# A depthwise convolution on GpSimd: each tap's product and sum in two halves of the row, in turn

## The chip, the cores and the metric

The kernel runs on one core of a Trainium2 chip. The metric is the device time of one execution in microseconds (us). A core has five engines that run their own instruction queues in order and meet only through semaphores: TensorE (PE), VectorE (DVE), ScalarE (ACT), GpSimd (POOL) and SyncE (SP), which here only issues transfers. Lower is better.

## The reference

One decoder layer over 1024 tokens of width 1024. An input projection feeds three mixers side by side: sparse attention (an indexer picks 256 keys for each query, then softmax attention), multi-scale pooling, and a convolution module. Their outputs are concatenated, projected, normalised, and go through a mixture of experts (top 2 of 16) with a second norm. The part that matters here is the convolution module on 256 channels, 31 taps wide:

```python
def conformer_conv(u, conv_w, conv_b, ln_g, ln_b):
    a, gate = jnp.split(u, 2, axis=-1)
    h = a * jax.nn.sigmoid(gate)
    h = lax.conv_general_dilated(h, conv_w, window_strides=(1,), padding=[(CONV_WIDTH - 1, 0)], ...
                                 feature_group_count=D_C) + conv_b
    h = layer_norm(h, ln_g, ln_b)
    return jax.nn.silu(h)
```

Each channel is filtered on its own: output(t) is the bias plus the sum over w of weight(w) times h(t + w - 30). Everything is float32.

## The kernel before, in words

Channels lie on partitions, tokens along the free dimension, so a tap w is a shifted read of a padded row: hpad[:, g, w:w + 1024] times one weight per partition. There are two groups g of 128 channels. Their inputs hpad are set by VectorE at the end of the input projection (L1393), and the result is conv[:, g, :], 1024 elements a partition.

Group 0: TensorE does taps 0 to 23 as matmuls with diagonal matrices (L740), ScalarE brings the result with the bias to conv[:, 0, :] (L1148, semaphore conv0), and GpSimd adds taps 24 to 30 (L1910 a product into the buffer tapped, L1911 a sum into conv; semaphore conv0_rest counts the sums).

Group 1: GpSimd does all 31 taps in the helper tap(w). Tap 0 is one instruction with product and bias (L1875). Taps 1 to 30 are a product into tapped (L1878) and a sum into conv (L1879), whose semaphore is conv1. The helper link() lets the engine wait for the instruction just issued. The product of tap w waits for the sum of tap w - 1, since it overwrites tapped, and the sum waits for its product.

GpSimd's queue in order: causal masks (L1859), taps 0 to 7 of group 1, the pooling mixer (L1885 to L1903), taps 8 to 30 of group 1, taps 24 to 30 of group 0, small tables for the router (L1916 to L1926), and much later the gathers and scatters of the experts and the additions of the last norm (L1986).

Beside the taps three things run. First the end of the projection with VectorE's split L1350 and 25 rounds of a search for the top-k threshold (L1444). Then, from about 250 us, the attention proper, whose order of steps is written out by attention_steps(): "qk" scores (TensorE L786), VectorE's bias and row maximum (L1532), ScalarE's exponential (L1155), transposes (TensorE L806, copies by ScalarE L1163 or VectorE L1541), and the product with the values (TensorE L819, ScalarE L1167). Between them VectorE fits seven "choose" instructions for each block of queries (L1476 to L1488) that turn the scores into a mask; several have two inputs in SBUF.

Who waits for the taps: near the end of the attention steps stand "split 0" and "cm". In "split 0" ScalarE waits for conv0_rest and conv1 (L1142, L1143) before it casts a first piece of mix (L1119). In "cm" TensorE waits for both (L838, L839) and sums conv over the channels for its norm (L841). VectorE then subtracts the mean (L1556). The steps behind them in each queue (the scores and products of the last pairs, and then the output projection) wait in order.

Of the kernel before, what the change touches and what calls it, by code (L numbers as in the profile page):

```python
# [17 lines left out]
S, D = 1024, 1024  # L18
# [4 lines left out]
TAPS = 31  # L23
# [47 lines left out]
TAPS_PE = 24  # L71
# [140 lines left out]
def program(nc, a):  # L212
    ctx = ExitStack()
    with ctx:
# [5 lines left out]
        def sem(name):  # L220
            return ctx.enter_context(nc.semaphore(name))
# [178 lines left out]
        def probs_at(u):  # L400
# [21 lines left out]
            sem(n) for n in ("diag_set", "conv0_mm", "conv0", "conv1", "pooled", "pool_chain"))  # L422
        conv0_rest, both_in, both_mm = sem("conv0_rest"), sem("both_in"), sem("both_mm")

# [219 lines left out]
        def _(pe):  # L644
# [116 lines left out]
            for step in STEPS:  # L761
# [46 lines left out]
                elif kind == "pv":  # L808
                    _, b, j, n = step
# [26 lines left out]
                elif kind == "cm":  # L836
                    _, c, r = step
                    pe.wait_ge(conv0_rest, TAPS - TAPS_PE)  # L838
                    pe.wait_ge(conv1, TAPS)  # L839
                    for i in range(2):  # L840
# [174 lines left out]
        def _(act):  # L1015
# [109 lines left out]
            for step in STEPS:  # L1125
# [14 lines left out]
                elif kind == "split":  # L1140
                    if step[1] == 0:
                        act.wait_ge(conv0_rest, TAPS - TAPS_PE)  # L1142
                        act.wait_ge(conv1, TAPS)  # L1143
                        act.wait_ge(ring_act, seen(RING_ACT, RING_OF["pw", 1, 1]))
# [698 lines left out]
        def _(pool):  # L1843
# [23 lines left out]
            def link(ins):  # L1867
                own[0] += 1
                ins.then_inc(pool_chain, 1)
                pool.wait_ge(pool_chain, own[0])  # L1870

            def tap(w):
                src, by = hpad[:, 1, w:w + S], convw[:, TAPS + w:TAPS + w + 1]
                if w == 0:
                    pool.tensor_scalar(conv[:, 1, :], src, by, convb[:, 1:2], ALU.mult, ALU.add).then_inc(conv1, 1)  # L1875
                else:
                    pool.wait_ge(conv1, w)
                    link(pool.tensor_scalar(tapped[:], src, by, None, ALU.mult))  # L1878
                    pool.tensor_tensor(conv[:, 1, :], conv[:, 1, :], tapped[:], ALU.add).then_inc(conv1, 1)  # L1879

# [26 lines left out]
            pool.wait_ge(conv0, 1)  # L1907
            pool.wait_ge(conv1, TAPS)
            for n, w in enumerate(range(TAPS_PE, TAPS)):
                link(pool.tensor_scalar(tapped[:], hpad[:, 0, w:w + S], convw[:, w:w + 1], None, ALU.mult))  # L1910
                pool.tensor_tensor(conv[:, 0, :], conv[:, 0, :], tapped[:], ALU.add).then_inc(conv0_rest, 1)  # L1911
                pool.wait_ge(conv0_rest, n + 1)

# [133 lines left out]
```

## Time and profile before

| | us |
|---|---|
| median of 3 runs (lowest to highest) | 1001.8 (1001.33 to 1005.58) |
| the profiled execution, whole | 1005.54 |
| its span, first to last instruction | 1003.6 |
| TensorE busy in the span | 912.2 (91%) |
| VectorE busy | 695.6 (69%) |
| ScalarE busy | 560.6 (56%) |
| GpSimd busy | 370.0 (37%) |
| GpSimd, products of taps L1878 and L1910 | 92.0 + 22.6 |
| GpSimd, sums of taps L1879 and L1911 | 74.4 + 17.8 |

The page's strip cuts the span into 40 slices of 25 us; a digit is the busy share in tenths:

```profile
PE   6999999999798789999936999999999999999980
DVE  5339888798899956636677767798888854334276
POOL 0000079999999992000001112122232221111136
PEclk9999999999899999999978999999999999999995
```

TensorE is nearly full all along; the stretch of GpSimd's taps is slices 6 to 16, about 130 to 381 us. An average over the span says little about a change of GpSimd's work; what counts is the stretch in which it runs and who waits for its end.

### The profile page before, as it was taken

Reading aid. Unit: us, or ns where it says so; the run is one execution under the profiler, and the core shown is the slowest. Engines: PE = TensorE matmul, PEld = TensorE weight load, DVE = VectorE, ACT = ScalarE, POOL = GpSimd, SP = SyncE. Lnnn points to the kernel's source line nnn. Section 1 sums busy time; section 2 is a strip of 40 time slices with the busy share of each in tenths; the row PEclk is TensorE's granted clock in tenths of the full one; section 3 lists DMA queues with packets and bytes.
Section 4 is the critical chain, followed back from the end, with each engine's and each line's share of the span. In section 5 each row is a group of like instructions: output and inputs, shape, how many; then the busy total and the mean of one; then the engine's idle time right before and its main releaser. Section 6 shows DMA issues by size and latency. Waiting matters only on the chain.

```text
span 1003.6 us, 15909 instructions
## 1 busy us (share of the span) xinstructions
PE 912.2 (91%) x4804; PEld 715.4 (71%) x4805; DVE 695.6 (69%) x1028; ACT 560.6 (56%) x805; POOL 370.0 (37%) x243
## 2 busy tenths in 40 slices
PE   6999999999798789999936999999999999999980
PEld 5877888744366567888825888888878888888760
DVE  5339888798899956636677767798888854334276
ACT  4256667686687566611141656778777744234342
POOL 0000079999999992000001112122232221111136
PEclk9999999999899999999978999999999999999995
DMA  8550111000000100242685679999999987652375
GB/s 234 135 141 22 42 43 64 1 0 2 1 1 1 44 1 22 93 151 69 256 335 210 214 221 330 383 400 403 384 403 396 391 293 248 199 146 43 107 243 206
DMA packets 63486, 172.54 MB, mean 172 GB/s; under 512 B 19297, under 2 KB 33633, under 8 KB 51120
## 3 DMA queue, kind: packets, MB, share of 16 engines
q1 hardware_dynamic: 55664, 143.85, 38.8%
q0 software_dynamic: 7488, 27.07, 10.9%
q10 hardware_dynamic: 288, 1.05, 0.3%
q8 instruction: 24, 0.39, 0.2%
q14 instruction: 22, 0.18, 0.1%
HBM read 142.79 MB, written 26.74 MB: 169 GB/s over the span
## 4 chain that ended last, share of the span: by engine, by line
PE 51%; DMA 4%; DVE 3%; issue 2%; ACT 2%; POOL 1%; DVEq 0%; POOLq 0%; ACTq 0%; SPq 0%
PE ps L467 14%; PE ps L469 14%; PE ps L468 14%; DMA raw<-in_w_gate 3%; PE ps L946 2%; PE ps L819 1%; PE ps L786 1%; POOL xb L1986 1%; PE ps L982 1%; PE ps L870 1%; DMA acc_d<-ysb,idx_add 1%; PE ps L806 1%; DVE xgT_lo L1761 0%; DVE wlo L1751 0%; DMA xg<-x_d,slot_token 0%
## 5 line engine op out<-in xcount | busy, mean ns | idle before, releaser
L1751 DVE TENSOR_TENSOR wlo<-raw,whi 128x2048 fp32r<-128x2048 f32 x96 | 216.2, 2288 | 52.1 <-ACT whi L1245 52.1
L1245 ACT CAST whi<-raw 128x2048 fp32r<-128x2048 f32 x96 | 180.2, 1911 | 48.2 <-PE ps L469 18.5
L467 PE MATMUL ps<-whi,xgT_hi 128*128 128x512 f32 x384 | 152.5, 397 | 6.2 <-DVE xgT_lo L1761 6.2
L469 PE MATMUL ps<-whi,xgT_lo 128*128 128x512 f32 x384 | 150.6, 392 | 0.0
L468 PE MATMUL ps<-wlo,xgT_hi 128*128 128x512 f32 x384 | 150.2, 391 | 0.0
L1878 POOL TENSOR_SCALAR tapped<-hpad,par 128x1024 f32<-128x1024 f32 x30 | 92.0, 3067 | 2.9
L467 PE MATMUL ps<-xT_hi,w_hi 128*128 128x512 f32 (+1 forms) x224 | 88.0, 393 | 1.9 <-DVE xT_lo L1357 1.9
L1954 POOL COPY idx_now<-slot_token 128x1 int32 (+1 forms) x24 | 8.1, 336 | 219.9 <-PE ps L946 219.9
L467 PEld LDWEIGHTS ps<-whi,xgT_hi 128*128 128x128 f32 x384 | 72.7, 189 | 22.4 <-issue 6.4
L468 PE MATMUL ps<-xT_lo,w_hi 128*128 128x512 f32 (+1 forms) x224 | 86.7, 387 | 0.0
L469 PE MATMUL ps<-xT_hi,w_lo 128*128 128x512 f32 (+1 forms) x224 | 86.6, 387 | 0.0
L469 PEld LDWEIGHTS ps<-whi,xgT_lo 128*128 128x128 f32 x384 | 72.5, 189 | 15.4
L468 PEld LDWEIGHTS ps<-wlo,xgT_hi 128*128 128x128 f32 x384 | 72.5, 189 | 14.5
L467 PE MATMUL ps<-whi,hT_hi 128*128 128x512 f32 x192 | 76.9, 401 | 0.5 <-issue 0.5
L1444 DVE TENSOR_SCALAR_CACHE_REDUCE junk_dve<-bias,sm 128x1024 bf16<-128x1024 f32 (+2 forms) x75 | 75.7, 1010 | 1.8
L1879 POOL TENSOR_TENSOR conv<-conv,tapped 128x1024 f32<-128x1024 f32 x30 | 74.4, 2480 | 2.5
L469 PE MATMUL ps<-whi,hT_lo 128*128 128x512 f32 x192 | 75.1, 391 | 0.0
L468 PE MATMUL ps<-wlo,hT_hi 128*128 128x512 f32 x192 | 74.9, 390 | 0.0
L1969 POOL DMA_INDIRECT acc_d<-ysb,idx_add x23 | 40.3, 1751 | 93.2 <-ACT ysb L1272 92.4
L1095 ACT ACTIVATE junk_act<-bias,sm 128x768 bf16<-128x768 f32 (+2 forms) x75 | 62.2, 829 | 14.7 <-DVE sm L1462 10.6
L1532 DVE CUSTOM_DVE_ANT_0 probs<-ps,bias 128x128 f32<-128x128 f32 (+7 forms) x64 | 45.9, 754 | 20.2 <-PE ps L786 17.5
L1155 ACT ACTIVATE probs<-probs,sm 128x128 f32<-128x128 f32 (+7 forms) x64 | 50.0, 781 | 14.0 <-DVE sm L1532 14.0
(328 smaller groups left out, 1818.4 us busy)
## 6 DMA issues: line engine op xcount, KB each, us to landing
raw<-in_w_gate SPq DMA_DIRECT2D x32, 1024.0 KB, 10.4
raw<-in_w_up SPq DMA_DIRECT2D x32, 1024.0 KB, 11.7
raw<-in_w_down SPq DMA_DIRECT2D x32, 1024.0 KB, 9.4
w_raw<-in_w_in SPq DMA_DIRECT2D x14, 512.0 KB, 3.9
x_tok<-in_x SPq DMA_DIRECT2D x8, 512.0 KB, 7.7
wo_raw<-in_w_o SPq DMA_DIRECT2D x16, 256.0 KB, 2.8
x_res<-in_x SPq DMA_DIRECT2D x16, 256.0 KB, 3.4
x_d<-xa SPq DMA_DIRECT2D x4, 512.0 KB, 6.1
```

Of the source, the lines that this page charges most:

```text
L467: pe.matmul(out, l_hi, r_hi, start=start, stop=False)
L468: pe.matmul(out, l_hi, r_lo, start=False, stop=False)
L469: return pe.matmul(out, l_lo, r_hi, start=False, stop=stop)
L1095: act.activation(junk_act[:, 0:WIDTH[b]], bias[:, AT[b]:AT[b] + WIDTH[b]], ACT.Sign, bias=cands[r % 2][:, c:c + 1], scale=-1.0, accum_out= ...
L1155: act.activation(row, row, ACT.Exp, bias=negmax[:, c:c + 1], scale=-1.0, accum_out=rowsum[:, c:c + 1]).then_inc(exped, 1)
L1245: act.copy(whi[:, n, :], raw[:, n, :]).then_inc(gu_hi if n < 4 else dn_hi, 1)
L1444: dve.tensor_scalar(junk_dve[:, 0:WIDTH[b]], bias[:, AT[b]:AT[b] + WIDTH[b]], now[:, c:c + 1], 0.0, ALU.is_lt, ALU.add, accum_out=res[:, c ...
L1532: dve.tensor_tensor_reduce(out=probs_at(u)[:, 0:WIDTH[b]], in0=scores_at(u, WIDTH[b]), in1=bias[:, AT[b]:AT[b] + WIDTH[b]], scale=-1.0, sc ...
L1751: dve.tensor_tensor(wlo[:, n, :], raw[:, n, :], f32(whi[:, n, :]), ALU.subtract).then_inc(gu_lo if n < 4 else dn_lo, 1)
L1878: link(pool.tensor_scalar(tapped[:], src, by, None, ALU.mult))
L1879: pool.tensor_tensor(conv[:, 1, :], conv[:, 1, :], tapped[:], ALU.add).then_inc(conv1, 1)
L1969: pool.indirect_dma_start(acc_d, bass.IndirectOffsetOnAxis(ap=idx_add[:], axis=0), ysb[:], None, compute_op=ALU.add).then_inc(y_out, 16)
```

## The change

Each tap but the 0th is done in two halves of 512 elements. Where there was one product and one sum, there are now product of half 0, product of half 1, sum of half 0, sum of half 1. A product of half c waits for the sum of half c of the tap before; a sum of half c waits for its own product. All of them count on two semaphores: tap_mul for products, conv1 for sums (tap 0 adds 2 to it, both groups count on it). The semaphore conv0_rest is gone, and the consumers wait for conv1 at its final value.

```diff
@@ TensorE, step "cm" @@
-                    pe.wait_ge(conv0_rest, TAPS - TAPS_PE)
-                    pe.wait_ge(conv1, TAPS)
+                    pe.wait_ge(conv1, 2 * (2 * TAPS - TAPS_PE))
@@ ScalarE, step "split" 0 @@
-                        act.wait_ge(conv0_rest, TAPS - TAPS_PE)
-                        act.wait_ge(conv1, TAPS)
+                        act.wait_ge(conv1, 2 * (2 * TAPS - TAPS_PE))
@@ GpSimd, tap(w) @@
                 if w == 0:
-                    pool.tensor_scalar(conv[:, 1, :], src, by, convb[:, 1:2], ALU.mult, ALU.add).then_inc(conv1, 1)
+                    pool.tensor_scalar(conv[:, 1, :], src, by, convb[:, 1:2], ALU.mult, ALU.add).then_inc(conv1, 2)
                 else:
-                    pool.wait_ge(conv1, w)
-                    link(pool.tensor_scalar(tapped[:], src, by, None, ALU.mult))
-                    pool.tensor_tensor(conv[:, 1, :], conv[:, 1, :], tapped[:], ALU.add).then_inc(conv1, 1)
+                    for c in range(2):
+                        half = slice(c * 512, (c + 1) * 512)
+                        pool.wait_ge(conv1, 2 * w - 1 + c)
+                        pool.tensor_scalar(tapped[:, half], src[:, half], by, None, ALU.mult).then_inc(tap_mul, 1)
+                    for c in range(2):
+                        half = slice(c * 512, (c + 1) * 512)
+                        pool.wait_ge(tap_mul, 2 * w - 1 + c)
+                        pool.tensor_tensor(conv[:, 1, half], conv[:, 1, half], tapped[:, half], ALU.add).then_inc(conv1, 1)
@@ GpSimd, taps 24 to 30 of group 0 @@
-            pool.wait_ge(conv1, TAPS)
+            pool.wait_ge(conv1, 2 * TAPS)
             for n, w in enumerate(range(TAPS_PE, TAPS)):
-                link(pool.tensor_scalar(tapped[:], hpad[:, 0, w:w + S], convw[:, w:w + 1], None, ALU.mult))
-                pool.tensor_tensor(conv[:, 0, :], conv[:, 0, :], tapped[:], ALU.add).then_inc(conv0_rest, 1)
-                pool.wait_ge(conv0_rest, n + 1)
+                for c in range(2):
+                    half = slice(c * 512, (c + 1) * 512)
+                    pool.wait_ge(conv1, 2 * (TAPS + n) - 1 + c)
+                    pool.tensor_scalar(tapped[:, half], hpad[:, 0, w + c * 512:w + (c + 1) * 512], convw[:, w:w + 1],
+                                       None, ALU.mult).then_inc(tap_mul, 1)
+                for c in range(2):
+                    half = slice(c * 512, (c + 1) * 512)
+                    pool.wait_ge(tap_mul, 2 * (TAPS + n) - 1 + c)
+                    pool.tensor_tensor(conv[:, 0, half], conv[:, 0, half], tapped[:, half], ALU.add).then_inc(conv1, 1)
```

## Rows read from the trace of the kernel before

**Rows 1.** Busy time by engine in one stretch (start:end, length, then each engine):

```profile
255.00:357.00 102.00, 84.51 (x720) 55.46 (x718) 96.73 (x160) 69.94 (x188) 98.83 (x35) 0.95 0.04 12
```

The engines are PE, PEld, DVE, ACT and POOL, each with its number of instructions; then PEclk, the DMA share and GB/s.

**Rows 2.** Timeline of GpSimd: start, duration (us), line, operation, out<-in.

```profile
130.63 1.19 POOL L1875 TENSOR_SCALAR conv<-hpad,par 128x1024 f32<-128x1024 f32 x1 [0.28 <-DVE hpad L1393]
...
213.58 2.84 POOL L1878 TENSOR_SCALAR tapped<-hpad,par 128x1024 f32<-128x1024 f32 x1
216.50 2.36 POOL L1879 TENSOR_TENSOR conv<-conv,tapped 128x1024 f32<-128x1024 f32 x1
218.96 2.84 POOL L1878 TENSOR_SCALAR tapped<-hpad,par 128x1024 f32<-128x1024 f32 x1
...
378.48 2.38 POOL L1911 TENSOR_TENSOR conv<-conv,tapped 128x1024 f32<-128x1024 f32 x1
380.94 0.22 POOL L1916 TENSOR_TENSOR fold<-ident 128x16 f32<-128x16 f32 x1
381.10 0.31 POOL L1917 MEMSET rw_wide<- 128x256 f32 x1
```

**Rows 3.** Timelines of TensorE and ScalarE where the taps' end is needed.

```profile
382.52 3.60 PE L841 MATMUL ps<-conv,ones_conv 128*128 128x512 f32 x8
...
383.00 1.04 ACT L1119 CAST mix_hi<-mix 128x1024 fp32r<-128x1024 f32 x1
```

**Rows 4.** GpSimd's groups by line: count | busy us, mean ns | idle before.

```profile
L1878 POOL TENSOR_SCALAR tapped<-hpad,par 128x1024 f32<-128x1024 f32 x30 | 92.0, 3067 | 2.9
L1879 POOL TENSOR_TENSOR conv<-conv,tapped 128x1024 f32<-128x1024 f32 x30 | 74.4, 2480 | 2.5
...
L1910 POOL TENSOR_SCALAR tapped<-hpad,par 128x1024 f32<-128x1024 f32 x7 | 22.6, 3231 | 0.8 <-POOL conv L1879 0.2
L1911 POOL TENSOR_TENSOR conv<-conv,tapped 128x1024 f32<-128x1024 f32 x7 | 17.8, 2538 | 0.6
...
L1899 POOL TENSOR_TENSOR doubled<-doubled,par 64x16 f32<-64x16 f32 x4 | 0.9, 216 | 0.3
...
L1925 POOL TENSOR_TENSOR rw_gain<-sm 128x128 f32<-128x128 f32 x1 | 0.4, 400 | 0.1
```

**Rows 5.** Timeline of GpSimd near the end: sums that don't wait for each other.

```profile
983.34 9.28 POOL L1986 TENSOR_TENSOR xb<-xb,ln_b 128x1024 f32<-128x1024 f32 x4
992.59 2.34 POOL L1986 TENSOR_TENSOR xg<-xg,ln_b 128x1024 f32<-128x1024 f32 x1
```

**Rows 6.** Timelines of VectorE and GpSimd over the same microseconds, in two places.

```profile
285.12 1.54 DVE L1480 SCALAR_TENSOR_TENSOR tied<-bias,sm,above 128x640 f32<-128x640 f32 x1
...
342.78 4.33 DVE L1482 TENSOR_TENSOR_SCAN tie_no<-tied 128x1024 f32<-128x1024 f32 x1
...
349.29 1.24 DVE L1484 SCALAR_TENSOR_TENSOR tied<-tie_no,sm,tied 128x1024 f32<-128x1024 f32 x1
350.56 3.26 DVE L1486 SCALAR_TENSOR_TENSOR tied<-tied,above 128x1024 f32<-128x1024 f32 x1
...
284.87 2.85 POOL L1878 TENSOR_SCALAR tapped<-hpad,par 128x1024 f32<-128x1024 f32 x1
...
345.06 4.70 POOL L1910 TENSOR_SCALAR tapped<-hpad,par 128x1024 f32<-128x1024 f32 x1
349.84 2.90 POOL L1911 TENSOR_TENSOR conv<-conv,tapped 128x1024 f32<-128x1024 f32 x1
```

**Rows 7.** VectorE's groups by line from 250 to 358 us.

```profile
L1486 DVE SCALAR_TENSOR_TENSOR tied<-tied,above 128x512 f32<-128x512 f32 (+5 forms) x6 | 11.6, 1928 | 0.1
L1480 DVE SCALAR_TENSOR_TENSOR tied<-bias,sm,above 128x512 f32<-128x512 f32 (+5 forms) x6 | 10.4, 1738 | 0.0
...
L1484 DVE SCALAR_TENSOR_TENSOR tied<-tie_no,sm,tied 128x512 f32<-128x512 f32 (+5 forms) x6 | 9.4, 1564 | 0.0
```

**Rows 8.** TensorE busy and its granted clock (PEclk, third number) in two windows.

```profile
328.00:332.00 4.00, 1.05 (x6) 0.92 0.00 0
332.00:336.00 4.00, 4.00 (x32) 0.65 0.01 4
```

More of the change, by code:

```diff
@@ L422, in program @@
             sem(n) for n in ("diag_set", "conv0_mm", "conv0", "conv1", "pooled", "pool_chain"))
-        conv0_rest, both_in, both_mm = sem("conv0_rest"), sem("both_in"), sem("both_mm")
+        tap_mul, both_in, both_mm = sem("tap_mul"), sem("both_in"), sem("both_mm")
         ring_mm, ring_act, ring_dve = sem("ring_mm"), sem("ring_act"), sem("ring_dve")
```

## The prediction

> **What bounds the kernel now.** I read the page's slices first and then one stretch, that of GpSimd's taps. GpSimd's strip is full from about 130 to 381 us and nearly empty elsewhere, so the change can act there alone. In the window over the attention part [rows 1] the reader is to see that from 255 to 357 us GpSimd is busy 98.8 of 102 us and VectorE 96.7, while TensorE has 84.5 and ScalarE 69.9: in this stretch VectorE (its scores, maxima and top-k choices) holds the pace and TensorE idles some 17 us. Behind that, on the page's chain of work, TensorE's matmuls follow each other with hardly a piece of another engine.
>
> The timeline of GpSimd [rows 2] shows the taps as one unbroken chain: a first tap at 130.63 us, then product and sum in strict turn, each waiting for the one before, until the last sum ends at 378.48 + 2.38 = 380.86 us. Who needs that end is in the code: TensorE's "cm" step (L838 to L841, sums over the convolved channels) and ScalarE's first "split" wait for all 37 products and sums, and each stands in order in its queue. The timeline of both [rows 3] shows TensorE's first L841 matmul at 382.52 us and ScalarE's cast at 383.00, neither behind a wait. The slack of the taps is thus 382.52 - 380.86 = 1.66 us: anything that lengthens GpSimd's chain by more is paid one for one by TensorE, and shortening it gives nothing beyond what TensorE itself can use. From 382 us on the chain that ended last is TensorE's nearly everywhere, and the transfers of the experts' weights are issued on events behind this point, so I let a shift at 382 us go through to the end undiminished.
>
> **The change, part by part.** It removes 37 products and 37 sums of 1024 elements a partition (30 taps on the second channel group, 7 on the first) and adds 74 of each at 512. A half's product now waits for the same half's sum of the tap before, and a sum for its own half's product, so that the instruction just ahead is never the one waited for. The 0th tap, the pooling between taps and the bytes moved stay.
>
> Step 1, a tap today. Undisturbed, 213.58 to 218.96 us is 5.38 us [rows 2]: product 2.84, gap 0.08, sum 2.36, gap 0.10. These are gaps of a dependent pair.
>
> Step 2, half lengths. The sum's fixed part comes from short ones [rows 4]: 16 elements take 216 ns, so 2360 ns at 1024 is 2.13 ns an element and 182 ns fixed; from the 128-element row (400 ns) the fixed part is 120 ns. Half a sum is 1.24 to 1.27 us. The single-operation product has no short row. I give it the sum's fixed 0.18 us, so half is 1.42 + 0.09 = 1.51 us; the bounds are none at all and nearly two thirds of it, see the third rival. Four instructions: 3.02 + 2.54 = 5.56 us.
>
> Step 3, the gaps. Where GpSimd's instructions don't wait for each other, the next starts before the last ends: the four sums of the last norm and the fifth start over 992.59 - 983.34 = 9.25 us, 2.31 each, with a duration of 2.34 [rows 5], an overlap of 0.03; the short pair at 380.94 and 381.10 overlaps by 0.06 [rows 2]. Four boundaries save 0.13 to 0.24 us beside the 5.56. A tap is then 5.32 to 5.43 us, 5.26 with the smaller fixed part: -0.12 to +0.05 us against today. I take the middle, -0.02, because the short and the long pair bound it evenly: 37 x -0.02 = -0.7 us, ends -4.4 and +1.9 us (no overlap at all would be +6.7). So the removed wait is worth about what the added starts cost.
>
> Step 4, the meeting with VectorE. The rows [rows 6] show the two engines in each other's way: VectorE's L1486 over 1024 elements took 3.26 us from 350.56, while the same kind of instruction, L1484, took 1.24 at 349.29. Its own 1.24 us can have begun only at 350.56 + 3.26 - 1.24 = 352.58, and the GpSimd sum it had met ran from 349.84 to 352.74. In turn GpSimd's product at 345.06 took 4.70 in place of 2.84, since the scan at 342.78 (4.33 us, itself held up by a sum) ran until 347.11. L1484 at 349.29 ran free beside the late part of that product (to 349.76), while L1480 at 285.12, over 640 elements, took 1.54 us where 0.78 would do: it got through at 285.88, 1.0 us after the start of the product at 284.87. So a sum blocks VectorE's two-input instructions for nearly all its time, a product only in its early part. The Trainium skill says the same more strictly (SBUF — State Buffer, Who interferes with whom): the loser waits for the whole instruction of the other. The trace agrees for sums and not for products.
> What this costs GpSimd today: the mean durations [rows 4] less the undisturbed 2.84 and 2.36 give 30 x (0.223 + 0.120) + 7 x (0.387 + 0.178) = 14.2 us. What it costs VectorE: the three three-operand groups [rows 7] are busy 31.4 us; 18 instructions over 3 x 4224 elements at 1.24 us per 1024 would be 15.3, so 16 us of waiting on these alone, more with the scans.
> With halves a VectorE instruction that meets a sum waits for half a sum, so its waits should fall to about half, 8 us or more off a stretch in which it sets the pace. GpSimd loses: today a VectorE instruction of about 1 us often fits into the 1.9 us in which a product leaves the way free; with two free pieces of about 0.95 us each it overruns into the next read. Over a tap's cycle I get 0.35 us of delay for each such instruction today and 0.54 after. With some 35 instructions that is +6.6 us; the even arrival it assumes is not what the rows show (VectorE's instructions queue up behind GpSimd's), so I take +5, bounds 0 and +8.
>
> Step 5, the sum. GpSimd's end moves by -0.7 + 5 = +4.3 us. Less 1.66 of slack, TensorE's cm step is 2.6 us late against today. VectorE's gain does not help: it brings TensorE to that step perhaps 8 us early, where it waits in order, with qk and pv of the next pair queued behind, and ScalarE behind its own wait. That idle time has a price: behind an idle piece (1.05 busy of 4 us) the granted clock was 0.92 and then 0.65 over 4 us in which TensorE was full [rows 8], 1.7 us lost in all. The cm matmuls would meet the same, +1.7 us, bounds 0 and their own 3.6 us [rows 3]. Together 2.6 + 1.7 = +4.3 us.
>
> The profiled execution took 1005.54 us, span 1003.6; changed it would be 1009.8. The runs have their median at 1001.8, 3.7 us below it; I carry the difference over unchanged: 1001.8 + 4.3 = 1006.1 us. The same difference says that the slack of 1.66 us may be smaller in other runs, if they are quicker ahead of 382 us.
>
> **The rivals.**
> First, the taps end earlier. If starts overlap by more than 0.06 us at half length and VectorE delays GpSimd no more than today, the tap is up to 0.2 us shorter and the end 0 to 7 us earlier. The slack (-1.66) and the clock's price (+1.7) cancel, so the kernel gains what GpSimd's end gains: VectorE's freed time has TensorE there early enough to use it. For it: VectorE is the pace setter and loses over 16 us to whole sums. Against it: step 3's overlaps are small. Time 995 to 1001.8 us; it decides from the point where the shorter tap outweighs the added delay by VectorE, 0.14 us a tap for +5.
> Second, on the slow side: VectorE finds no opening. Today every GpSimd instruction is followed by a gap in which a blocked VectorE instruction gets in. If back-to-back halves leave none, it waits through Sa, Sb and a product's read instead of one sum, its waits double (+16 us and more on the groups of [rows 7]), and TensorE reaches cm late. Place: L1480 to L1488 between 255 and 357 us; it decides once the extra waits pass TensorE's 17 us of idleness there, or GpSimd's end. Time 1011 to 1026 us. No row shows back-to-back GpSimd reads beside such VectorE instructions.
> Third, the product's cost isn't in its length. The 0th tap, a product with an added bias over the same 1024 elements, took 1.19 us [rows 2], the plain product 2.84. If the plain one also moves its data in 1.0 us, some 1.8 are fixed, a half takes 2.3 us, a tap is 1.7 us longer and 37 of them are +63 us: about 1065 us. Against it: L1480 found the way shut for the product's first 1.0 us [rows 6], so the reading stands at its start, which a fixed part ahead of the data would not give; a fixed part behind it isn't excluded. The Trainium skill (GPSIMD Engine Reference, Engine selection) calls one-input operations roughly line-rate, which speaks for this rival; the row of 2.84 us disagrees.
> Fourth, the change doesn't do what it says: the halves follow each other with today's dependent gaps of 0.09 us. A tap is 5.56 + 0.36 = 5.92, 37 x 0.54 = +20 us: about 1022 us.
>
> **How the numbers follow.** Forecast 57%: GpSimd ends 0 to 9 us later, 1001.8 to 1011; of that 20 points lie over +5 us. First rival 24%, of which 13 points are faster by over 5 us. Second 8%, third 6%, fourth 5%. A change under 0.5% (5 us) can hardly be told from none here, since three runs spread over 4 us. Faster 0.13, same 0.37 + 0.11 = 0.48, slower 0.20 + 0.19 = 0.39. The range goes from 996.0, which leaves out 9 of the first rival's points, to 1021, which leaves out the third rival and 5 points of the second and fourth: 20 in all.
>
> **What would show it.** GpSimd's lines: 74 products near 1.51 us and 74 sums near 1.27 undisturbed, four starts in 5.3 to 5.4 us; a product near 2.3 is the third rival, gaps of 0.09 the fourth. GpSimd's last half sum near 385 us, TensorE's L841 starting within 0.2 us of it behind a wait on it, of some 10 us, at a granted clock below 1. L1480 to L1488 busy 8 us less or more confirms step 4, more busy than today is the second rival. The forecast is wrong if L841 isn't behind the taps, or if the part behind 390 us doesn't take its time of today.

## The result, and the profile after

| | before | after |
|---|---|---|
| median, us | 1002.6 (4 runs, 1001.33 to 1005.58) | 1014.2 (4 runs, 1013.87 to 1015.66) |
| ratio, 95% interval | | 1.0109 [1.0085, 1.0133] |
| profiled execution, its span | 1005.54, 1003.6 | 1013.87, 1011.5 |
| first tap starts | 130.63 | 127.63 |
| last sum of the taps ends | 380.86 | 388.21 |
| first cm matmul starts | 382.52, behind no wait | 388.35, behind a wait of 17.97 |

The changed kernel is slower by 1.1%. One execution of those that follow, of whole rows with the product ahead, ran with TensorE's granted clock at 0.555 throughout and took 1559.42 us; it is left out of the ratios. In the changed kernel the lines have moved by a few: products are L1878 and L1916, sums L1882 and L1921, the cm matmuls L840, ScalarE's first cast L1118, VectorE's choose instructions L1474 to L1486.

The slices of the page after, to be held against the four rows of before: GpSimd's strip is full from slice 6 to 15 and has a 4 in slice 16 where it had a 2, and TensorE's has a 5 and a 6 in slices 15 and 16 (about 354 to 405 us) where it had an 8 and a 9.

```profile
PE   6999999999899856999955999999999999999990
DVE  5249888898899633637678766698988854334276
POOL 0000099999999994000001112123133221111237
PEclk9999999999999987899976999999999999999995
```

The timeline of GpSimd after (start, duration, line, operation; x2 is two instructions printed as one row, an undisturbed tap being two such rows, and the last rows are the end of the taps) answers to [rows 2]:

```profile
127.63 1.20 POOL L1873 TENSOR_SCALAR conv<-hpad,par 128x1024 f32<-128x1024 f32 x1 [0.35 <-DVE hpad L1391]
...
207.46 3.11 POOL L1878 TENSOR_SCALAR tapped<-hpad,par 128x512 f32<-128x512 f32 x2
210.53 2.51 POOL L1882 TENSOR_TENSOR conv<-conv,tapped 128x512 f32<-128x512 f32 x2
213.00 3.11 POOL L1878 TENSOR_SCALAR tapped<-hpad,par 128x512 f32<-128x512 f32 x2
216.08 2.51 POOL L1882 TENSOR_TENSOR conv<-conv,tapped 128x512 f32<-128x512 f32 x2
218.56 1.57 POOL L1878 TENSOR_SCALAR tapped<-hpad,par 128x512 f32<-128x512 f32 x1
...
349.36 3.11 POOL L1916 TENSOR_SCALAR tapped<-hpad,par 128x512 f32<-128x512 f32 x2 [0.16 <-POOL conv L1882]
...
385.71 2.50 POOL L1921 TENSOR_TENSOR conv<-conv,tapped 128x512 f32<-128x512 f32 x2
```

The two taps from 207.46 to 218.56 us take 5.55 us each, where one took 5.38 [rows 2]. That is the first thing to see: the tap is longer even where nothing disturbs it. The second is the start of both chains: the profiled execution of before had its first tap 3.0 us later than the one of after. So the end of the taps moved by 388.21 - 380.86 = 7.35 us on the page, but the chain itself grew from 380.86 - 130.63 = 250.23 to 388.21 - 127.63 = 260.58 us, by 10.35.

GpSimd's groups after, from 120 to 400 us (count | busy us, mean ns of one | idle before), answer to [rows 4]:

```profile
L1878 POOL TENSOR_SCALAR tapped<-hpad,par 128x512 f32<-128x512 f32 x60 | 101.6, 1705 | 0.2
L1882 POOL TENSOR_TENSOR conv<-conv,tapped 128x512 f32<-128x512 f32 x60 | 83.8, 1418 | 0.0
L1916 POOL TENSOR_SCALAR tapped<-hpad,par 128x512 f32<-128x512 f32 x14 | 21.9, 1582 | 0.2 <-POOL conv L1882 0.2
L1921 POOL TENSOR_TENSOR conv<-conv,tapped 128x512 f32<-128x512 f32 x14 | 17.6, 1285 | 0.0
```

The timelines of TensorE and of ScalarE after, where they need the taps, answer to [rows 3]:

```profile
369.72 0.66 PE L827 MATMUL ps<-ident,rlrep 128*128 128x128 f32 x4
388.35 6.05 PE L840 MATMUL ps<-conv,ones_conv 128*128 128x512 f32 x8 [17.97 <-POOL conv L1921]
394.33 1.99 PE L786 MATMUL ps<-keyT,qT 64*128 64x512 f32 x8
...
388.24 1.04 ACT L1118 CAST mix_hi<-mix 128x1024 fp32r<-128x1024 f32 x1 [17.44 <-POOL conv L1921]
```

TensorE stood at cm from 370.38 us, 12.1 us earlier than in [rows 3], and waited 17.97 us. Its eight matmuls then took 6.05 us in place of 3.60. The windows over this place (start:end, length, then PE, PEld, DVE, ACT and POOL with their counts, PEclk, DMA share, GB/s; the first window is that of [rows 1]):

```profile
255.00:357.00 102.00, 92.27 (x812) 62.70 (x812) 84.14 (x159) 76.09 (x199) 101.84 (x65) 0.97 0.04 12
...
370.00:388.00 18.00, 0.38 (x4) 0.14 (x2) 1.21 (x2) 0.81 (x2) 18.00 (x14) 0.57 0.00 0
388.00:392.00 4.00, 3.65 (x5) 1.61 (x6) 2.16 (x2) 1.56 (x2) 3.35 (x9) 0.50 0.02 4
392.00:396.00 4.00, 4.00 (x13) 1.46 (x11) 2.57 (x4) 0.00 (x0) 0.00 (x0) 0.86 0.21 66
396.00:400.00 4.00, 3.68 (x46) 3.02 (x44) 2.66 (x5) 1.73 (x4) 0.00 (x0) 1.00 0.00 0
```

Two things stand in them. In the first window VectorE is busy 84.1 us where it was 96.7, and TensorE 92.3 where it was 84.5 [rows 1]: that part of the kernel did get quicker. And the clock is at 0.50, the lower of TensorE's two levels (1.2 GHz), while the engine is full from 388 us, and back at 1.00 from 396.

VectorE's groups after, from 250 to 358 us, answer to [rows 7]:

```profile
L1480 DVE TENSOR_TENSOR_SCAN tie_no<-tied 128x512 f32<-128x512 f32 (+5 forms) x6 | 11.9, 1984 | 0.1
L1484 DVE SCALAR_TENSOR_TENSOR tied<-tied,above 128x512 f32<-128x512 f32 (+5 forms) x6 | 8.7, 1454 | 0.1
L1482 DVE SCALAR_TENSOR_TENSOR tied<-tie_no,sm,tied 128x512 f32<-128x512 f32 (+5 forms) x6 | 7.6, 1273 | 0.0
L1478 DVE SCALAR_TENSOR_TENSOR tied<-bias,sm,above 128x512 f32<-128x512 f32 (+5 forms) x6 | 7.0, 1161 | 0.0
```

The three three-operand groups are busy 8.7 + 7.6 + 7.0 = 23.3 us, where they were 31.4.

### The profile page after: what moved, and what is told of

The parts are those of the page before. It is cut to its first block, busy times and chain, and to the rows that moved or that the text cites. A ratio compares the mean times of both kernels' runs of the same rounds, so it can differ in the third digit from the quotient of the medians.

```text
span 1011.5 us, 15981 instructions
## 1 busy us (share of the span) xinstructions
PE 911.8 (90%) x4804; PEld 716.1 (71%) x4805; DVE 684.6 (68%) x1028; ACT 560.6 (55%) x805; POOL 387.4 (38%) x317
## 3 DMA queue, kind: packets, MB, share of 16 engines
q0 software_dynamic: 7488, 27.07, 10.9%
q10 hardware_dynamic: 288, 1.05, 0.3%
## 4 chain that ended last, share of the span: by engine, by line
PE 50%; POOL 26%; DMA 11%; DVE 7%; issue 3%; ACT 2%; DVEq 0%; ACTq 0%; POOLq 0%; SPq 0%
PE ps L467 14%; PE ps L469 14%; PE ps L468 14%; POOL tapped L1878 10%; DMA raw<-in_w_gate 10%; POOL conv L1882 8%; POOL tapped L1916 2%; DVE wlo L1749 2%; POOL conv L1921 2%; PE ps L945 1%; POOL doubled L1896 1%; DVE bias L1403 1%; POOL doubled L1903 1%; PE ps L711 1%; DVE sm L1595 1%
## 5 line engine op out<-in xcount | busy, mean ns | idle before, releaser
L1878 POOL TENSOR_SCALAR tapped<-hpad,par 128x512 f32<-128x512 f32 x60 | 101.6, 1705 | 0.2
L1882 POOL TENSOR_TENSOR conv<-conv,tapped 128x512 f32<-128x512 f32 x60 | 83.8, 1418 | 0.0
L468 PEld LDWEIGHTS ps<-wlo,xgT_hi 128*128 128x128 f32 x384 | 72.2, 188 | 14.2
L1094 ACT ACTIVATE junk_act<-bias,sm 128x768 bf16<-128x768 f32 (+2 forms) x75 | 62.2, 829 | 15.1 <-DVE sm L1460 11.1
L1260 ACT ACTIVATE silu<-ps 128x512 f32<-128x512 f32 x24 | 14.3, 595 | 76.6 <-PE ps L469 76.6
```

The lines of the kernel that those rows point to most:

```text
L468: pe.matmul(out, l_hi, r_lo, start=False, stop=False)
L1094: act.activation(junk_act[:, 0:WIDTH[b]], bias[:, AT[b]:AT[b] + WIDTH[b]], ACT.Sign, bias=cands[r % 2][:, c:c + 1], scale=-1.0, accum_out= ...
L1878: pool.tensor_scalar(tapped[:, half], src[:, half], by, None, ALU.mult).then_inc(tap_mul, 1)
L1882: pool.tensor_tensor(conv[:, 1, half], conv[:, 1, half], tapped[:, half], ALU.add).then_inc(conv1, 1)
```

## The experiments

The first theory, from these rows: the length of GpSimd's chain sets the end, since it is 10 us longer while TensorE comes 9 us earlier (12.1 less the 3.0 us of the earlier start); what VectorE wins from the halves is real, but is spent waiting at cm. Its rival: the slower time comes from elsewhere (more instructions, the clock, VectorE), and the wait at cm only shows it. A second question is why VectorE wins: because a half is short, or because of the order in which the halves come.

Where a table or a text below says "three groups" it is the busy time of the three groups above from 250 to 358 us, and "cm after the first tap" is the start of the first cm matmul less that of the first tap, which takes the early or late start of an execution out.

**The load on GpSimd and TensorE.** One constant was changed, in the kernel before and in the one after: TensorE does three more taps of group 0 and GpSimd three fewer.

```diff
-TAPS_PE = 24
+TAPS_PE = 27
```

On the changed kernel:

> The changed kernel with 27 in place of 24 taps of group 0 on TensorE, 4 instead of 7 on GpSimd. Theory A (the changed kernel lost because GpSimd's end holds up step cm by 18 us, while VectorE's freed time had TensorE there 9 us early): GpSimd ends 3 x 5.56 = 16.7 us earlier, TensorE has 6 matmuls of 0.45 us more, it waits next to nothing, and the time falls by 16 us to about 998 us, 4 to 6 us below the kernel before. Rival (the halves cost elsewhere too, not only at this wait): the time stays above 1003 us.

On the kernel before:

> Control to the run with 27 taps: the kernel before with the same three taps moved from GpSimd to TensorE. Theory A (TensorE was not waiting for GpSimd, its pace up to 357 us is VectorE's, which whole-length sums hold up): GpSimd ends 16 us earlier without use, TensorE has 2.7 us more matmuls just ahead of the scores, so 1002 to 1005 us, minus at most 3 us by less meeting of GpSimd and VectorE near 355 us. Rival (GpSimd's end held this kernel too): 3 us or more faster than before.

The first took 1000.73 us, ratio to before 0.9974 [0.9952, 0.9996]; the second 1010.99 us, ratio 1.0064 [1.0036, 1.0091]. The timeline of TensorE shows the cm matmuls of the first at 374.85 us, at their undisturbed 3.6 us and without a wait, as GpSimd's last sum had ended at 370.5. So taking away three taps took 13.5 us off the changed kernel: the wait at cm is its price, and the first theory holds. The same edit made the kernel before slower, though GpSimd was done at 359.4 us, 29 us ahead of cm at 388.0: it gained nothing from an earlier end and paid for the taps on TensorE, with VectorE's three groups at 32.5 us. That is a miss upward, as 1002 to 1005 us had been expected: the last tap matmuls ahead of the attention (L740) take 15.73 us for 36 where they took 10.58 for 24, so the three taps cost TensorE 5.2 us there and not 2.7. Cm is 8.2 us later after the first tap than in the kernel before; where the other 3 us went wasn't looked into. Eight of the ten executions took 1010.7 to 1013.1 us and two 1003.3 and 1004.4, and why isn't known. The pair is also the cleanest measure of what the halves give VectorE, since in neither do the taps hold anything up: cm comes 247.2 us after the first tap with halves and 260.1 without, and the kernel is 0.9% faster.

**The order of the halves.** Product, sum, product, sum, each waiting for the one ahead of it, so that only the lengths are those of the change:

```diff
                     for c in range(2):
                         half = slice(c * 512, (c + 1) * 512)
-                        pool.wait_ge(conv1, 2 * w - 1 + c)
+                        pool.wait_ge(conv1, 2 * w + c)
                         pool.tensor_scalar(tapped[:, half], src[:, half], by, None, ALU.mult).then_inc(tap_mul, 1)
-                    for c in range(2):
-                        half = slice(c * 512, (c + 1) * 512)
                         pool.wait_ge(tap_mul, 2 * w - 1 + c)
```

> Halves as in the changed kernel, but in the order product, sum, product, sum, each waiting for the instruction just ahead. It tells what the interleaving is worth apart from the length. Theory A (added starts cost 6.4 us, the interleaving only hides a gap of about 0.12 us at each of 4 boundaries): an undisturbed tap of 5.56 + 4 x 0.12 = 6.0 us, GpSimd's end 37 x 0.48 = 18 us behind that of the changed kernel, time 1014 + 17 = 1031 us. Theory B (the interleaving matters for more, since dependent halves open the way to VectorE between any two): the tap is 6.0 us too, but VectorE's three-operand groups are faster than in the changed kernel by some us more. Rival: the waits cost nothing and the tap stays 5.56 us, time 1014 us.

1029.34 us, ratio 1.0254 [1.0221, 1.0287]. The timeline of GpSimd in this kernel:

```profile
213.71 1.57 POOL L1878 TENSOR_SCALAR tapped<-hpad,par 128x512 f32<-128x512 f32 x1
215.36 1.27 POOL L1880 TENSOR_TENSOR conv<-conv,tapped 128x512 f32<-128x512 f32 x1
216.73 1.56 POOL L1878 TENSOR_SCALAR tapped<-hpad,par 128x512 f32<-128x512 f32 x1
218.38 1.27 POOL L1880 TENSOR_TENSOR conv<-conv,tapped 128x512 f32<-128x512 f32 x1
219.75 1.56 POOL L1878 TENSOR_SCALAR tapped<-hpad,par 128x512 f32<-128x512 f32 x1
```

The same four instructions take 6.04 us instead of 5.55: gaps of 0.08 and 0.10 us stand where the changed kernel overlaps by 0.03. So the interleaving does what it says, 0.49 us a tap. In this order a tap in halves costs 0.66 us more than a whole one (6.04 against 5.38), and the interleaving hides three quarters of it. VectorE's three groups are busy 24.3 us here, nearly the 23.3 of the changed kernel. With these products it is the length of the halves that frees VectorE, not their order.

**The interleaving alone, with whole rows.** Products and sums of 1024 elements, with three buffers for products, so that from tap 8 on a product is issued ahead of the sum it doesn't need. The core of the edit:

```diff
+            def product(n):
+                g, w = todo[n]
+                if n > 2:
+                    pool.wait_ge(conv1, TAPS_FIRST + n - 2)
+                pool.tensor_scalar(ahead[n % 3][:], hpad[:, g, w:w + S], ...
+                                   None, ALU.mult).then_inc(tap_mul, 1)
...
+                pool.tensor_tensor(conv[:, g, :], conv[:, g, :], ahead[n % 3][:], ALU.add).then_inc(conv1, 1)
```

> The kernel before, whole lengths, but from tap 8 on with three product buffers and each product issued one ahead of the sum before it, so that no instruction waits for the one just ahead (30 of 37 taps). It isolates the wait that the change wanted to hide. Theory A (an independent start saves 0.10 to 0.13 us at each of two boundaries): tap 5.38 - 0.24 = 5.14 us undisturbed, GpSimd's end 7 us earlier, near 371 us when it starts at 128, and the time that of before, 1000 to 1004 us, since TensorE didn't wait for it. Rival (without gaps VectorE finds no opening between whole instructions): VectorE's three-operand groups busier than 31 us, TensorE late at step cm, 1006 us or more.

1004.47 us, ratio 1.0002 [0.9967, 1.0036]. The rows are those of another run of the same kernel:

> The kernel with products one ahead once more, for a profile at TensorE's usual clock. Theory A (a removed wait is worth 0.12 us a boundary, and TensorE didn't wait for GpSimd): undisturbed tap 5.14 us, step cm without a wait, some 1003 us. Rival (the gaps were VectorE's openings): three-operand groups of VectorE busier than their 31 us of the kernel before, and step cm later by as much.

One time, 1003.81 us. A tap takes 5.15 us in it (213.20 to 218.35), 0.23 less than before, the last sum ends at 373.6 and the cm matmuls start at 380.8, behind no wait. The gaps are gone and GpSimd is done 7 us ahead of cm, and the kernel isn't faster: VectorE's three groups are busy 32.8 us (31.4 before), and cm comes 253.1 us after the first tap (251.9 before). A shorter chain on GpSimd is worth nothing by itself here.

**The product's cost.** The prediction's third rival turned on tap 0, a product with an addition that took 1.19 us while the plain product took 2.84. Here every product, whole as before, also adds 0.0:

```diff
-                    link(pool.tensor_scalar(tapped[:], src, by, None, ALU.mult))
+                    link(pool.tensor_scalar(tapped[:], src, by, 0.0, ALU.mult, ALU.add))
```

> The kernel before with one edit: each product is multiply, then add 0.0, in place of multiply alone; whole length. Tap 0, which multiplies and adds, took 1.19 us for the 1024 elements for which the plain product takes 2.84. Theory A (the two-operation form has a quicker path): product 1.2 us, a tap of 3.7, GpSimd's end 37 x 1.65 = 61 us earlier, near 320 us. TensorE's step cm is then nowhere near waiting, and the kernel gains only what VectorE gets back in its stretch, up to the 17 us of TensorE's idle time there: 990 to 1000 us. Rival (tap 0 is quick because both of its scalars come from memory, or because its source is aligned): product 2.84 us as before, time 1002 us.

998.22 us, ratio 0.9952 [0.9928, 0.9975]. GpSimd's timeline in this kernel:

```profile
210.14 2.36 POOL L1879 TENSOR_TENSOR conv<-conv,tapped 128x1024 f32<-128x1024 f32 x1
212.60 1.12 POOL L1878 TENSOR_SCALAR tapped<-hpad,par 128x1024 f32<-128x1024 f32 x1
213.80 2.35 POOL L1879 TENSOR_TENSOR conv<-conv,tapped 128x1024 f32<-128x1024 f32 x1
```

The product takes 1.12 us. The taps end at 312.7 us, 68 us sooner than before, and the kernel gains 5. VectorE's three groups are at 26.4 us: it meets none of GpSimd's instructions after 313. Up to there its waits are no shorter than before: what the 18 instructions of the three groups took over their undisturbed lengths is an estimated 11 us, all of it ahead of 313, where the kernel before has 10 us ahead of 313 and 6 behind.

**Both together.** The changed kernel with the quick products:

```diff
-                        pool.tensor_scalar(tapped[:, half], src[:, half], by, None, ALU.mult).then_inc(tap_mul, 1)
+                        pool.tensor_scalar(tapped[:, half], src[:, half], by, 0.0, ALU.mult, ALU.add).then_inc(tap_mul, 1)
```

> The changed kernel (halves in turn) with each product as multiply, then add 0.0. Theory A (both effects are separate: the quick form takes GpSimd's end out of the way, halves shorten VectorE's waits): half products of 0.65 us, a tap of 3.7 to 3.8 us, GpSimd's end near 330 us, TensorE at step cm near 370 us without a wait as in the changed kernel (370.4), so 9 us under before: about 993 us, and 4 us under whole-length quick products. Rival (VectorE gains nothing further, since quick products leave less of GpSimd's time free between sums): 998 us, that of the whole-length quick products.

1006.02 us, ratio 1.0036 [1.0014, 1.0058]. That is a miss: slower than whole rows with the same products (0.9952), although the taps end at 323.5 us and no one waits for them. VectorE's three groups are busy 30.1 us. A timeline of VectorE and one of GpSimd over the same microseconds in this kernel show one of its long waits:

```profile
282.97 2.81 DVE L1484 SCALAR_TENSOR_TENSOR tied<-tied,above 128x384 f32<-128x384 f32 x1
...
281.06 1.75 POOL L1878 TENSOR_SCALAR tapped<-hpad,par 128x512 f32<-128x512 f32 x2
282.79 2.49 POOL L1882 TENSOR_TENSOR conv<-conv,tapped 128x512 f32<-128x512 f32 x2
285.25 1.75 POOL L1878 TENSOR_SCALAR tapped<-hpad,par 128x512 f32<-128x512 f32 x2
```

L1484 over 384 elements takes 0.51 us undisturbed (L1486 at 275.60 us in the trace of before). Here it took 2.81, so it worked from 285.27 on: it had waited through both half sums, 282.79 to 285.28, and got in only as the products began. Three more of the 18 instructions of the three groups waited 2.2 us or more in this way, at 256.33, 261.26 and 278.19 us. This is the prediction's second rival, VectorE finding no opening between two instructions that follow without a gap. The test for it is to put the gaps back, with the quick products kept: the chained order of the first experiment and the addition of 0.0.

> Halves with quick products (multiply, then add 0.0), in the order product, sum, product, sum, each waiting for the one just ahead. Beside it stand the same halves in turn (1006 us), where VectorE's two-input instructions waited 2.2 to 2.8 us, longer than a half. Theory A (back-to-back halves pass the way on to each other when products are short; a dependent gap opens it to VectorE): no wait of VectorE's much over 1.3 us, its five choose groups 10 us less busy than in that run, GpSimd's end near 340 us and harmless, TensorE at cm near 370 us: 991 to 996 us, the fastest so far. Rival (short products themselves are at fault, since they leave VectorE fewer free stretches): the groups stay as busy, 1002 to 1007 us.

997.28 us, ratio 0.992 [0.989, 0.995]. The three groups fall from 30.1 to 22.6 us, and cm comes 243.9 us after the first tap instead of 253.5, though each tap is longer, 4.29 us against 3.80. That this costs GpSimd half a microsecond a tap doesn't matter, since the taps end at 346.0.

But the edit changes two things at once: it puts a gap behind each half, and it parts the two sums by a product. No run here has the one without the other, so which of them lets VectorE in is not shown. More rows of the kernel without gaps, VectorE and then GpSimd, in two places:

```profile
153.14 7.55 DVE L1348 TENSOR_TENSOR w_lo<-w_raw,w_hi 128x1024 fp32r<-128x1024 f32 x1 [0.61 <-ACT w_hi L1019]
...
153.22 2.55 POOL L1882 TENSOR_TENSOR conv<-conv,tapped 128x512 f32<-128x512 f32 x2
155.74 1.37 POOL L1878 TENSOR_SCALAR tapped<-hpad,par 128x512 f32<-128x512 f32 x2
157.07 2.54 POOL L1882 TENSOR_TENSOR conv<-conv,tapped 128x512 f32<-128x512 f32 x2
...
315.88 1.68 DVE L1482 SCALAR_TENSOR_TENSOR tied<-tie_no,sm,tied 128x768 f32<-128x768 f32 x1
...
315.49 1.26 POOL L1921 TENSOR_TENSOR conv<-conv,tapped 128x512 f32<-128x512 f32 x1
316.71 1.98 POOL L1921 TENSOR_TENSOR conv<-conv,tapped 128x512 f32<-128x512 f32 x1
```

L1348 takes 1.23 us where nothing is in its way. Here it ended at 160.69, so it had waited 6.3 us, past two half sums, two products and two more half sums: the products between the sums did not let it in, which speaks for the gap. Against a rule without exception stands L1482 at 315.88 us. It needs about 0.95 us, so it worked from about 316.6 on, as the first half sum ended, and the second half sum grew from 1.27 to 1.98 us: VectorE got in between two sums that had no gap.

**More taps on GpSimd.** The freed time of GpSimd can take taps from TensorE. With TAPS_PE = 18, on halves in the change's order and on whole rows, both with quick products:

> As the run before it, but with 18 taps of group 0 on TensorE and 13 on GpSimd. Theory A (27 taps on TensorE cost 5 us of its time in front of the attention, and GpSimd now has some 40 us to spare): GpSimd's end 6 x 3.75 = 22 us later, near 353 us, still ahead of cm; TensorE loses 12 matmuls of 0.45 us, 5.4 us, just in front of the scores: about 987 us. Rival (VectorE's search, done near 247 us, sets the start of the attention): within 2 us of the run before it.

> The kernel before, whole lengths, quick products, 18 taps on TensorE. With the run before it, it tells what halves are worth once GpSimd is out of the way. Theory A (halves shorten VectorE's waits): 4 us above the run before it, about 991 us. Rival (halves worth nothing here): the same time as that run.

1007.56 us, ratio 1.0046 [1.0018, 1.0074], and 1002.55 us, ratio 1.0004 [0.9982, 1.0027]: two misses by 20 and 12 us. On whole rows it is slower than with 24 taps (0.9952); on halves the intervals overlap (1.0036 with 24). GpSimd then works longer beside VectorE's choose instructions (three groups 31.4 and 31.5 us), and TensorE stood for 7.7 us in either behind ScalarE's conv0 (L1146 and L1148), which the shorter work of TensorE had it reach early. With TAPS_PE = 22, chained halves and then whole rows:

> The run before it with 22 taps of group 0 on TensorE, 9 on GpSimd. In the run with whole quick products ScalarE waited 2.88 us for TensorE's taps before it could bring the convolution out, while with 18 taps TensorE waited for ScalarE instead. Two taps fewer take 1.8 us off TensorE there: 1 to 2 us under the run before it. Rival: less than 0.5 us, if the search's end sets the start anyway, or 1 to 2 us more, if the 9 us of added GpSimd work meet VectorE's choose instructions.

> Whole rows, products as a multiply and an addition of 0.0, no halves, and TAPS_PE = 22 in place of 24 (two more taps of a channel tile on GpSimd than in the kernel before). Against e10, which has the same products, the same 22 and chained halves, only the length of GpSimd's instructions differs. Tap 3.66 us by e2's trace, against 4.29 in the chained halves: GpSimd has more room here than there. Theory A (short instructions with a gap behind each give VectorE its openings, and that is what e9 had over e2): VectorE's groups of three-operand instructions keep their waits (31 us or more for the three largest after the scan, e10 had 22.8), the search is later, and the time is 2 to 4 us over e10's: 996 to 998. Rival (the halves gained nothing, TensorE's load set e10's time): 992 to 995, GpSimd being done earlier. Decides between them: the ratio against e10's 0.989, and VectorE's groups in the stretch from 250 to 358.

993.44 us, ratio 0.9889 [0.9848, 0.9929], the fastest of all here, and 997.37 us, ratio 0.9937 [0.9918, 0.9957]. VectorE's groups in the chained halves, and then on whole rows, show the difference between them:

```profile
L1484 DVE SCALAR_TENSOR_TENSOR tied<-tied,above 128x512 f32<-128x512 f32 (+5 forms) x6 | 8.2, 1370 | 0.1
L1482 DVE SCALAR_TENSOR_TENSOR tied<-tie_no,sm,tied 128x512 f32<-128x512 f32 (+5 forms) x6 | 8.2, 1362 | 0.0
L1478 DVE SCALAR_TENSOR_TENSOR tied<-bias,sm,above 128x512 f32<-128x512 f32 (+5 forms) x6 | 6.4, 1074 | 0.0
```

```profile
L1486 DVE SCALAR_TENSOR_TENSOR tied<-tied,above 128x512 f32<-128x512 f32 (+5 forms) x6 | 9.9, 1651 | 0.1
L1484 DVE SCALAR_TENSOR_TENSOR tied<-tie_no,sm,tied 128x512 f32<-128x512 f32 (+5 forms) x6 | 9.1, 1516 | 0.0
L1480 DVE SCALAR_TENSOR_TENSOR tied<-bias,sm,above 128x512 f32<-128x512 f32 (+5 forms) x6 | 8.4, 1403 | 0.0
```

22.8 us against 27.4, and cm 239.8 against 248.3 us after the first tap. The 31 us that the theory asked for on whole rows weren't reached, the time of 996 to 998 was. The two intervals overlap a little, so the 4 us between the medians rest on these rows as much as on the times. Whether 22 is better than 24 with chained halves (0.9889 against 0.992) the runs don't tell: the intervals overlap widely.

The profiled executions side by side. P and S are product and sum, "dep" that each instruction waits for the one ahead:

| kernel | tap, us | taps end | three groups | cm after first tap | ratio |
|---|---|---|---|---|---|
| before (whole, dep) | 5.38 | 380.9 | 31.4 | 251.9 | 1 |
| after (halves PPSS) | 5.55 | 388.2 | 23.3 | 260.7, waited 18.0 | 1.0109 |
| after, 27 taps on TensorE | 5.54 | 370.5 | 22.0 | 247.2 | 0.9974 |
| before, 27 | 5.39 | 359.4 | 32.5 | 260.1 | 1.0064 |
| halves PSPS, dep | 6.04 | 408.4 | 24.3 | 277.4, waited 33.0 | 1.0254 |
| whole, product ahead | 5.15 | 373.6 | 32.8 | 253.1 | 1.0002 |
| quick, whole, dep | 3.66 | 312.7 | 26.4 | 246.5 | 0.9952 |
| quick, halves PPSS | 3.80 | 323.5 | 30.1 | 253.5 | 1.0036 |
| quick, halves PSPS, dep | 4.29 | 346.0 | 22.6 | 243.9 | 0.992 |
| the same, 22 taps on TensorE | 4.29 | 357.2 | 22.8 | 239.8 | 0.9889 |
| quick, whole, dep, 22 | 3.66 | 322.8 | 27.4 | 248.3 | 0.9937 |
| quick, halves PPSS, 18 | 3.80 | 351.9 | 31.4 | 255.9 | 1.0046 |
| quick, whole, dep, 18 | 3.66 | 338.9 | 31.5 | 251.8 | 1.0004 |

Only where cm waited do the taps decide. Of the rest, those with 30 us or more in the three groups reach cm 251.8 us or more after the first tap, those with 27.4 or less within 249.

## Why the prediction was right or wrong

The time lies in the range, the sign of the forecast was right, and so was the chain of reasons: the taps' end is what the change lengthens, VectorE's gain brings TensorE to cm early, it waits there, and the clock falls. The size was too small: +4.3 us forecast, +11.6 between the medians (the ratio gives +10.9). That the time lies in the range is in part luck: the forecast's own band was 1001.8 to 1011 us, and 1014.2 lies above it, in the band of the second rival (1011 to 1026), which isn't what made this kernel slower. By its steps:

**Slack at cm.** 1.66 us, used as the forecast said. Chain +10.35, less 1.66, plus 2.45 for the cm matmuls, is +11.1 us. The profiled spans differ by 7.9; with the 3.0 us by which the taps of before began later it is 10.9. So the sum closes, and nothing behind cm gave time back, as had been assumed. What the prediction had taken from this was wrong in one point: it carried the 3.7 us between the profiled execution and the median over to the changed kernel, and feared that the slack might be smaller in quick executions. The profiled execution of before lost 3.0 us ahead of its first tap. That moves the taps' end and TensorE's arrival at cm alike and leaves the slack as it is, and the changed kernel's profiled execution had no such loss (1013.87 us, its median 1014.2).

**Steps 2 and 3, the tap in halves: this is the step that failed.** It said -0.02 us a tap, -0.7 in all, with ends of -4.4 and +1.9 and +6.7 if nothing overlapped. It is +0.17 a tap, 37 x 0.17 = +6.3. Two terms were mis-sized. The product's fixed part was taken from the sum, 0.18 us, for want of a short product; it is 2 x 1.57 - 2.84 = 0.30, which is 0.12 us a tap. And the overlap of neighbours is 0.03 us each (3.11 for two of 1.57), the lower of the two rows it was taken between; the middle of both had been used, 0.07 us a tap too much. (The middle of the prediction's own -0.12 and +0.05 is -0.035 and not -0.02; that is 0.6 us over 37 taps, and to the wrong side.) Together 0.19 x 37 = 7.0 us, nearly the whole miss. The half sum, 1.27 us, was right.

**Step 4, the meeting with VectorE.** For VectorE: 8 us or more off the three groups was forecast, 8.1 came. For GpSimd: +5 was forecast. The means of the groups less the undisturbed 1.57 and 1.27 give 60 x (0.135 + 0.148) + 14 x (0.012 + 0.015) = 17.4 us, where before lost 14.2: +3.2. Most of what is left of the chain's 10.35 after 6.3 and 3.2 is one sum of 16 elements in the pooling, L1902 at 173.26 us, which took 1.08 us in place of 0.22. The start and end of the stretches tell where it fell: taps 0 to 7 grew by 1.4 us, the pooling by 0.85, taps 8 to 30 by 10.8, and the last seven took 2.7 us less than before, because VectorE, ahead of its old time, was done with its last block at 342.5 us and met none of them, while before it lengthened five of their instructions, from the sum at 342.24 to that at 356.62 us; [rows 6] has two of them.

**Step 5, the clock.** Forecast 1.7 with bounds 0 and 3.6, measured 6.05 - 3.60 = 2.45. The 1.7 itself was read a little high: 0.3 of it is the clock of 0.92 over 4 us in which TensorE was busy for 1.05 alone, so the rows gave some 1.5. The wait was to be some 10 us and was 17.97: 9.1 us by which TensorE was early (forecast 8), the taps' 10.35 and the slack's -1.66 make 17.8.

**The first rival** (the taps end earlier) was wrong already in the undisturbed tap. **The third** (the product's cost isn't in its length) as well: the plain half takes 1.57 us and not 2.3. What it had rested on, the 1.19 us of tap 0, had another cause, which the experiment with the added 0.0 brought out: it is the form of the instruction. The Trainium skill (GPSIMD Engine Reference, Engine selection) has one-input operations at roughly line-rate; the trace agrees for the form with two operations and not for that with one. **The fourth** (dependent gaps) is the chained experiment, whose undisturbed tap is 6.04 us; the rival had 5.92.

**The second rival** (no opening) did come about in the changed kernel, once, and cost nothing there. VectorE and then GpSimd:

```profile
243.94 3.08 DVE L1464 SCALAR_TENSOR_TENSOR sm<-sm 128x6 f32<-128x6 f32 x1
...
243.83 2.50 POOL L1882 TENSOR_TENSOR conv<-conv,tapped 128x512 f32<-128x512 f32 x2
```

The last part of the threshold search, over 6 elements, took 3.08 us in place of 0.17, past both half sums; but 4 us later VectorE stood 3.01 us for TensorE anyway. In the three groups no instruction waited much over 1.0 us (the longest is 1.52 against 0.51 us, at 268.62), less than half of what two half sums take. In the same order of halves with quick products such waits came often and cost time. What makes the difference between the two isn't settled. In both, two half sums follow each other with the same overlap; only the products ahead of them differ, 1.57 us each against 0.69. The prediction's own row reading, that a plain product leaves the way free after its first microsecond, would let VectorE start its instructions beside products and meet fewer sums, but it doesn't say why the choose instructions that met a first half sum got in ahead of the second in the one kernel and several did not in the other. The Trainium skill (SBUF — State Buffer, Who interferes with whom) has the loser wait for the whole of the other's instruction; the row at 282.97 us of the experiment shows a wait for two, and the row at 153.14 one for six.

## What to carry to other kernels

Before cutting an instruction into halves, find a row of the same operation at a short length: the fixed part differs between operations (0.30 us here for a product, 0.18 for a sum), and over 37 repetitions a tenth of a microsecond is 3.7 us. What a cut gives to the other engine (8 us here) counts only if the cut engine still ends in time, so pair the cut with moving work away from that engine: the same halves that cost 1.1% stood 0.9% ahead of whole rows where both kernels had three taps moved. Where two engines get in each other's way, try short instructions that wait for each other as well as back-to-back ones: with the quick products they were 1.2% faster (ratio 0.992 against 1.0036), though GpSimd's own chain was longer. Whether the gaps or the changed order did it isn't separated here.

## What the runs showed of the hardware

GpSimd's product of 1024 float32 elements by one scalar per partition takes 2.84 us as a single multiply and 1.12 us as a multiply and an addition of 0.0; at 512 elements 1.57 and 0.69. Adding the second operation makes it 2.3 to 2.5 times as quick.

Back-to-back instructions of GpSimd can keep VectorE out through more than one: a wait of 2.3 us behind two half sums of 1.27, and one of 6.3 us behind six instructions. They don't always: in the same kernel VectorE got in between two half sums at 316.7 us. With the halves in the order product, sum, product, sum and gaps of 0.08 to 0.10 us behind each, the three groups went from 30.1 to 22.6 us.

After TensorE had stood for 18 us its clock was at the lower level, 0.50, for the first 4 us of full work and 0.86 in the next 4; the eight matmuls that fell into it took 6.05 us in place of 3.60. In the chained experiment, after 33 us, the eight took 6.75 us, and the granted clock was 0.58 over the first 8 us.
